# Attention over frames in a two-layer encoder: score and value steps issued in pairs

## The reference, cut to what matters

```python
def mla_block(args):                       # 128 queries against all earlier keys, 8 heads
    mask = key_chunk[None, :] <= q_chunk[:, None]
    return _mla_attend(ql_i, qr_i, ckv, kr, mask)
...
s = (einsum('bqhl,bkl->bhqk', q_lat, ckv) + einsum('bqhr,bkr->bhqk', q_rope, kr)) * MLA_SCALE
p = softmax(where(mask, s, NEG_INF)); o = einsum('bhqk,bkl->bqhl', p, ckv)
...
o_band = _swa_attend(qc, k_band, v_band, sinks, key_mask)   # 64 queries against 144 to 208 keys
```

## Time and profile before

| what | before |
|---|---|
| median of three runs | 3037.05 us |
| profiled execution | 3030.18 us |
| its span on the core | 3028.4 us |
| PE (TensorE, matmul) busy | 2849.8 us, 94% of the span |
| DVE (VectorE) busy | 2136.6 us, 71% |
| ACT (ScalarE) busy | 1255.8 us, 41% |
| POOL (GpSimd) busy | 1725.3 us, 57% |

### The profile page before, as it was taken

The page is one execution under the profiler, slowest core; times in us unless marked ns, Lnnn a source line. Parts: engine busy times, 40 slices in busy tenths (PEclk is TensorE's granted clock), DMA queues, the critical chain, the costliest instruction groups (busy, mean ns, idle before and its releaser), DMA issues. The chain is left out here.

```text
span 3028.4 us, 53962 instructions
## 1 busy us (share of the span) xinstructions
PE 2849.8 (94%) x20172; PEld 2609.0 (86%) x20172; DVE 2136.6 (71%) x3858; ACT 1255.8 (41%) x2508; POOL 1725.3 (57%) x1380
## 2 busy tenths in 40 slices
PE   7989997999999999999989799969999999999997
PEld 7966665887999999999989666658889999999997
DVE  7757777658677767778654676757577777678876
ACT  3334345445344434444333344445453444344442
POOL 2323333437777767788632233334377777678875
PEclk9989999999999999999989799979999999999998
DMA  5331115543233343233322211155432333433331
GB/s 182 125 95 44 46 51 157 170 156 119 99 108 110 112 170 120 105 105 109 127 95 97 87 43 43 47 167 156 163 117 96 111 111 108 181 112 105 112 105 56
DMA packets 192126, 335.02 MB, mean 111 GB/s; under 512 B 56457, under 2 KB 111849, under 8 KB 189793
## 3 DMA queue, kind: packets, MB, share of 16 engines
q1 hardware_dynamic: 165680, 276.61, 27.9%
q10 hardware_dynamic: 17248, 29.82, 2.6%
q0 software_dynamic: 8976, 25.70, 2.2%
HBM read 262.98 MB, written 65.03 MB: 108 GB/s over the span
## 5 line engine op out<-in xcount | busy, mean ns | idle before, releaser
L1690 POOL TENSOR_TENSOR wopl<-T,woph 128x512 fp32r<-128x512 f32 x348 | 523.4, 1523 | 104.1 <-ACT woph L2184 102.7
L1631 POOL TENSOR_TENSOR Pl<-Pf,Ph 128x256 fp32r<-128x256 f32 (+5 forms) x174 | 219.2, 1267 | 374.2 <-DVE Ph L2633 374.2
L3108 PE MATMUL PS<-hidh,wdh 128*128 128x320 f32 (+2 forms) x1408 | 418.8, 297 | 6.8 <-DVE hidl L2922 4.8
L3110 PE MATMUL PS<-hidh,wdl 128*128 128x320 f32 (+2 forms) x1408 | 418.7, 297 | 0.0
L3109 PE MATMUL PS<-hidl,wdh 128*128 128x320 f32 (+2 forms) x1408 | 417.9, 297 | 0.0
L2184 ACT ACTIVATE woph<-T 128x512 fp32r<-128x512 f32 x348 | 216.7, 630 | 477.0 <-DVE T L2917 268.4
L3108 PE MATMUL PS<-xoh,woph 128*128 128x320 f32 x1232 | 383.1, 311 | 3.7 <-DVE xol L2826 1.8
L3110 PE MATMUL PS<-xoh,wopl 128*128 128x320 f32 x1232 | 381.5, 310 | 0.0
L3109 PE MATMUL PS<-xol,woph 128*128 128x320 f32 x1232 | 380.9, 309 | 0.0
L2975 DVE TENSOR_TENSOR acc<-acc,PS 128x320 f32<-128x320 f32 (+2 forms) x608 | 274.3, 453 | 150.5 <-PE PS L3110 147.6
L3108 PE MATMUL PS<-x_both,woph 128*128 128x264 f32 (+1 forms) x1232 | 348.3, 283 | 0.0
(11 more groups left out here) (508 smaller groups left out, 7698.7 us busy)
## 6 DMA issues: line engine op xcount, KB each, us to landing
ru<-in_W_FF SPq DMA_DIRECT2D x88, 512.0 KB, 4.3
rd<-in_W_FF SPq DMA_DIRECT2D x176, 256.0 KB, 2.6
rg<-in_W_FF SPq DMA_DIRECT2D x82, 512.0 KB, 4.2
sqt_scratch<-sqTs POOLq DMA_DIRECT2D x18, 512.0 KB, 4.2
hc<-out_H SPq DMA_DIRECT2D x18, 512.0 KB, 3.6
dkraw<-in_CKVT SPq DMA_DIRECT2D x16, 520.0 KB, 4.6
QS<-sqt_scratch SPq DMA_DIRECT2D x16, 512.0 KB, 3.3
mt<-mix_scratch SPq DMA_DIRECT2D x16, 512.0 KB, 4.5
```

The costliest lines, as they stand in the source:

```text
L1631: ins = pool.tensor_tensor(Pl[i][0:kk, 1, c], Pf[i][0:kk, 1, c], f(Ph[i][0:kk, 1, c]), ALU.subtract)
L1690: pool.tensor_tensor(wopl[k][:, :, :], w_whole(w, k, first), f(woph[k][:, :, :]), ALU.subtract)\
L3108: pe.matmul(out, wh, mh, start=start, stop=False)
L3110: return pe.matmul(out, wl, mh, start=False, stop=stop)
```

## The change

Steps are now taken two at a time. For an even n the list has: the scores of n + 2 and n + 3; up to two (`EARLY`) of the fill-ins at the front of the queue, if they use half the array; the split of n + 2; the values of n and of n + 1; the split of n + 3; the other fill-ins of both steps, those of the half array last unless a later item of the pair (`sc` for `sx`, `mc` for `mx`) needs them. Where step n is the last of its pass, the values of n + 1 come behind the whole-array fill-ins of the pair, as far as there are any. The windows of fill-ins end at an odd step. The slots of the ring are found by their number.

```diff
-            u["frees"] = rings[-RINGS] if len(rings) >= RINGS else None
+            u["frees"] = ([v for v in rings if v["r"] == u["r"]] or [None])[-1]
...
-        todo, at = merged(j + 1), window[j]
+        todo, at = merged(j + 1), window[j][:len(window[j]) - (window[j][-1] + 1) % 2]
...
-    for n in range(len(steps) + 2):
-        if n + 2 < len(steps):
-            put("st", **{k: v for k, v in steps[n + 2].items() if k != "kind"})
-        for kind, more in fills[n]:
-            put(kind, **more)
-        if n + 1 < len(steps):
-            put("sp", n=n + 1)
+    def halves_last(items):
+        got = []
+        for q, item in enumerate(items):
+            if item[0] not in ("sx", "mx") or ({"sx": "sc", "mx": "mc"}[item[0]] in [later[0] for later in items[q:]]):
+                got.append(item)
+        return got + [item for item in items if item not in got]
+    def values(n):
         if n < len(steps):
             put("pv", n=n)
             if steps[n]["last"]:
                 put("ox", x=steps[n]["x"], n=n)
+    for n in range(0, len(steps) + 2, 2):
+        for k in (n + 2, n + 3):
+            if k < len(steps):
+                put("st", **{key: v for key, v in steps[k].items() if key != "kind"})
+        todo, q = fills[n] + fills[n + 1], 0
+        while q < len(todo) and q < EARLY and todo[q][0] in ("sx", "mx"):
+            put(todo[q][0], **todo[q][1])
+            q += 1
+        if n + 2 < len(steps):
+            put("sp", n=n + 2)
+        values(n)
+        apart = n < len(steps) and steps[n]["last"]
+        todo = halves_last(todo[q:])
+        if not apart:
+            values(n + 1)
+        if n + 3 < len(steps):
+            put("sp", n=n + 3)
+        for kind, more in todo:
+            if apart and kind in ("sx", "mx"):
+                values(n + 1)
+                apart = False
+            put(kind, **more)
+        if apart:
+            values(n + 1)
```

More of the change, by code:

```diff
@@ L166 @@
 RINGS = 3
+EARLY = 2
 def chunks_of(t):
@@ L241, in plan_frames @@
         put("st", **{k: v for k, v in steps[n].items() if k != "kind"})
-    put("sp", n=0)
+    for n in (0, 1):
+        put("sp", n=n)
     window = {}
@@ L245, in plan_frames @@
         window.setdefault(u["x"] // 2, []).append(n)
-    fills = {n: [] for n in range(len(steps) + 3)}
+    fills = {n: [] for n in range(len(steps) + 4)}
     for j in range(NPASS // 2 - 1):
-        todo, at = merged(j + 1), window[j]
+        todo, at = merged(j + 1), window[j][:len(window[j]) - (window[j][-1] + 1) % 2]
         for q, item in enumerate(todo):
```

## The result

| | before | after |
|---|---|---|
| median (runs) | 3035.55 us (4) | 3126.74 us (4) |
| lowest to highest | 3031.37 to 3038.91 | 3124.13 to 3131.34 |
| profiled execution: time | 3030.2 us | 3124.55 us |
| profiled execution: span | 3028.4 us | 3122.8 us |

The ratio is 1.0302 (95% interval 1.0286 to 1.0318): the change costs 91 us, where 36 were forecast, and the time lies above the top of the range (3100). The direction was right, the size was not. One execution of the later run e10_copies_first took 4610.94 us at a granted clock of 0.552 and stays out of its comparison.

A forecast was written before the change was run, and what follows sets the result against it. PE sets the frames stage's pace, DVE close behind. Terms sum to +15.5 us per layer, +31 for two, plus 5 for clock: 36, taking the profiled 3030.2 to 3066 and the median to 3073; range 3042 to 3100.

The forecast's parts named there:

- ends of passes: Next pass's first values wait for ACT's accumulator copies, queued behind an exponential: +16.0 us per layer.
- string of maxima: In 5-step passes, DVE's reductions get later with added splits, so the transposes wait: +8.0 us per layer.
- copies QR: First score of odd passes waits 1.2 instead of 1.64 us for the maxima row's copies: -1.8 us per layer.
- even passes: Projection and transposes stand right before the first M score, which waits for ACT's copies: +4.0 us per layer.
- band tile, key projection: Band tile shift and key projection run as blocks with new waits: +2.0 and +4.5 us per layer.
- waits for Pl: Splits stand a whole pair ahead of their values, so these waits shrink: -5 us per layer, between 0 and -13.
- changes of form: Switches between scores and values on PE fall from 166 to 90 per layer, 0.16 us each: -12.2 us per layer.
- clock: Lower granted clock on PE after new waits in the frames stage: +5 us, bounds 0 and 18.
- two such dips: Two low-clock stretches after waits in the frames stage, like the earlier one costing 2.3 us: +5 us together.
- the clock follows every one of the eight strings: Rival: PE's clock falls at all eight maxima strings in the frames stage: 3086 us, chance 0.18.
- Even: Rival: only pass ends cost (32 us); form changes and Pl waits repay them, DVE having slack: 3035, chance 0.08.
- Faster: Rival: all Pl waits and form-change costs saved, pass ends cost only 2 x 8 us: 3002, chance 0.12.

The follow-up runs named there:

- e10_copies_first: Kernel before, with ScalarE's two copies of the maxima row moved ahead of the exponential that stood before them: 3031.33 us, ratio 0.9989.
- e4_clock: Kernel after, order unchanged, with 104 useless matmuls per layer added where TensorE would wait: 3089.72 us, ratio 1.0196.
- e3_even: Kernel after, with the values' projection and the maxima transposes moved between the pair's two band scores: 3127.55 us, ratio 1.0320.
- e8_before_clock: Kernel before, with useless matmuls in odd passes, three before the first mx and six before the first score: 3029.91 us, ratio 0.9986.
- e11_copies_clock: Kernel before, with ScalarE's two maxima copies moved ahead of an exponential and three useless matmuls in each of two odd-pass waits: 3027.11 us.

## Why the prediction was right in direction and wrong in size

Each term as it was put down, and what the runs show:

| term | forecast, both layers | shown, both layers (waits: PE's idle time in the stage) |
|---|---|---|
| ends of passes | +32 | waits on oT 15.0 us per layer, none before: +30; undoing them gives 34.5, a part of it clock |
| string of maxima | +16 | waits on mm 10.1 per layer, none before: +20; DVE 11.8 us for 11.0 forecast; undoing gives 23.7, a part of it clock |
| copies QR | -3.6 | waits 6.6 per layer to 0.2 and 0.6: -12 |
| even passes | +8 | waits for VHl (L2600) 6.8 and 6.7 for 1.4 and 0.5: +12; each 2.07 to 2.12 in the place named, for the 1.9 forecast |
| band tile, key projection | +13 | es, mxs, mxc, VHh, QNl new, less those for QR (L1948) and a slot: +21 |
| waits for Pl | -10 | 4.7 per layer to none: -9 |
| changes of form | -24.4 | 0.112 instead of 0.16: -17 |
| clock | +5, at most 18 | 50 us |

The two halves of the first table tell how the error divides. **The waits** came to +62 us of idle time; the forecast's terms for them (all but form and clock) sum to 2 x 27.7 = +55. By their rows they come to +61, which leaves next to nothing of the idle time unnamed. They were a good estimate: the mechanism and the places held, and so did the sizes of the two largest. That the sum is within 7 us has some luck in it, since the copies QR (9 us too little taken off) stood against the string, the even passes and the band tile (4, 4 and 8 too small). In the even passes I had named the QR copies and the profile names VHl; before step 20 the second copy ends at 300.22 and VHl at 300.27 us, so it is both. **The busy time** was forecast at 5 - 24 = -19 us and came to +35. Of these 54 us, 7 are the **price of a change of form**, which I had read as the gap and the late second pair together from a few rows. The others are the **clock term**, 5 forecast and 50 by e4_clock; 34.6 + 17 = 52 is what the busy time itself leaves for it.

So the step that failed is this one: "but much of what runs slowly there is paced by DVE anyway. I take two such dips, +5, bounds 0 and 8 x 2.3 = 18". It was wrong in the count and in the cover, not in the price. It counted the strings alone, eight in all, while the waits at the ends of passes and of even passes, which I had priced myself at 1.65 to 2.35 us, are of the same size and have their own low stretches: four in the period shown, 37 in the two stages against 8 before. And it let DVE cover all but two of them, though the string ends with mm: what follows is PE's work for which DVE waits (5.76 us). The 2.3 us for one low stretch were near: 50 us over 29 more stretches are 1.7 each. The reading behind the term was loose too. The stretch of the earlier trace rows has only the wait of 0.89 us at the head of its string before it, so it was no measure of what longer waits would do. The period from step 36 to 54 took 85.25 us (377.23 to 462.48), not the 75 forecast; with the clock held, in e4_clock, the same steps took 80.4, and had some of the added work in them.

The rival "the clock follows every one of the eight strings" (3086, chance 0.18) had the right mechanism, and shared the wrong count: it is 41 us under the result. (3037 + 31 + 18 with its price of forms at the low bound is 3097; the range ended at 3100.) "Even" needed DVE to have slack in the string, and it had almost none: 0.70 us in the 11.8 of the string, and mm last. "Faster" counted 27 us for the Pl waits, as the weight loads show them (13.3 to 0.4 per layer), of which PE itself had idled 9; the forms gave 17 for its 24. It fell because the new waits (30, 20, 12 and 21 us in the table) came to far more than the 34 us from which it gave up. The pair's lead does remove the waits for Pl; but the items that it gathers leave other places bare.

## What to carry to other kernels

Grouping work by kind on an engine that runs in order buys 0.11 us per change of form and takes away the covers under the chains that ran between the groups, so list for each such chain (copy out, reduction then transposes, projection then copy) what stands over it in the new order, before counting the changes saved. Here a new wait of about 2 us on PE cost its own length and some 0.8 of it again (50 us for 62) through the lower clock that followed; price it so, look whether the other engines really cover the slow stretch, and look where a wait removed alone may come back, as in e3_even. The only gains over the kernel before were small: 3 us by a move on a helper engine's queue that shortens one wait and nothing else (e10_copies_first), 4 by a few useless matmuls (e8_before_clock), each at the edge of what the runs tell, and 7 by both (e11_copies_clock).

## What was not expected of the hardware

Matmuls without use, put into PE's waits, pay: 208 of them (53 us of PE's time) made the kernel 37 us faster, and even in the kernel before, whose clock was 0.98 and 0.96 in the stage, 72 of them gave 4 us (between 1 and 8 by the interval). And DVE's subtraction of 128x512, 0.78 us in the mean, took 2.86 us in e3_even beside two subtractions of POOL in a row; what the two share no run here shows.
